# Quadrant products for the block-diagonal state-space matrices of a hybrid decoder layer, with its decode sums, attention split and row moves rearranged

## The reference

```python
x = x + 0.5 * swiglu(rmsnorm(x), w_gate, w_up, w_down)          # D_FF = 5504
z = rmsnorm(x) @ w_in          # q, k, v: 12 heads of 128; u: 1024; gate_a, gate_s: 2048
A = merged dilated attention of three head groups, 4 x 128 wide
# branch B: 64 channel groups of 16 channels, each drives one complex state of 64
bu = einsum('blgc,gpc->lbgp', u, bbar)                           # complex
x_s[l] = a * x_s[l-1] + bu[l]                                    # associative scan
y = Re(einsum('lbgp,gcp->blgc', x_s, c)) + d_skip * u
zs = gelu(y);  s_out = zs * sigmoid(zs @ glu_w + glu_b)
x = x + (sigmoid(gate_a) * (A @ w_attn_branch) + sigmoid(gate_s) * (s_out @ w_ssm_branch)) @ w_out
x = x + 0.5 * swiglu(rmsnorm(x), ...)                            # a second FFN
```

## Time and profile before

| | |
|---|---|
| median of 3 runs | 2301.75 us (2300.42 to 2302.45) |
| the profiled execution, its own time | 2301.55 us |
| its span, first to last instruction | 2299.8 us |
| mean granted TensorE clock | 0.998 |
| PE busy | 2272.1 us, 99% |
| DVE busy | 1404.6 us, 61% |
| ACT busy | 995.0 us, 43% |
| POOL busy | 535.9 us, 23% |

### The profile page before, as it was taken

How to read it: one execution, slowest core, us unless ns; L and a number is a source line. 1 busy time by engine, 2 the same in 40 slices (tenths; PEclk the granted TensorE clock), 3 DMA queues, 4 the chain that set the end, 5 groups by cost and what they waited for, 6 DMA issues and landing times.

```text
span 2299.8 us, 47445 instructions
## 1 busy us (share of the span) xinstructions
PE 2272.1 (99%) x18546; PEld 2255.7 (98%) x18546; DVE 1404.6 (61%) x1414; ACT 995.0 (43%) x1219; POOL 535.9 (23%) x565
## 2 busy tenths in 40 slices
PE   7999999999999999999999999999999999999999
PEld 7999999999999999999999999999999999999998
DVE  6566457775455667886657777655554455544555
ACT  5644333333344543444445555444433344333442
POOL 3795026650000204664405540110000000000000
PEclk9999999999999999999999999999999999999999
DMA  7888777777777688758848865568787777657864
GB/s 209 265 246 284 227 242 248 256 260 246 236 238 224 202 262 260 229 180 284 300 145 307 283 197 186 174 202 270 239 243 224 241 246 250 219 184 222 246 199 139
DMA packets 435222, 535.65 MB, mean 233 GB/s; under 512 B 27744, under 2 KB 415832, under 8 KB 431272
## 3 DMA queue, kind: packets, MB, share of 16 engines
q1 hardware_dynamic: 420224, 511.58, 70.7%
q0 software_dynamic: 3216, 11.75, 1.5%
q10 hardware_dynamic: 11680, 10.91, 1.4%
HBM read 510.95 MB, written 109.10 MB: 270 GB/s over the span
## 4 chain that ended last, share of the span: by engine, by line
PE 87%; DVE 5%; POOL 3%; issue 2%; DMA 1%; ACT 1%; SPq 0%; ACTq 0%; DVEq 0%
PE pa L1313 28%; PE pa L1314 27%; PE pa L1315 27%; DVE w_lo L927 2%; POOL c_exp L1781 1%; DVE head_sd L1088 1%; POOL pre L1777 1%; DMA raw<-in_ffn_w_up 1%; PE pb L1411 1%; PE pb L1586 1%; ACT w_hi L586 1%; PE pb L1571 1%; DVE up_v L1092 0%; DMA raw<-in_ffn_w_gate 0%; DVE xg_lo L934 0%
## 5 line engine op out<-in xcount | busy, mean ns | idle before, releaser
L927 DVE TENSOR_TENSOR w_lo<-raw,w_hi 128x1024 fp32r<-128x1024 f32 x736 | 937.0, 1287 | 643.9 <-ACT w_hi L586 639.3
L1313 PE MATMUL pa<-xg_hi,w_hi 128*128 128x264 f32 x3968 | 1137.5, 287 | 9.1 <-DVE w_lo L927 5.8
L1314 PE MATMUL pa<-xg_lo,w_hi 128*128 128x264 f32 x3968 | 1129.1, 285 | 0.0
L1315 PE MATMUL pa<-xg_hi,w_lo 128*128 128x264 f32 x3968 | 1127.9, 284 | 0.0
L586 ACT ACTIVATE w_hi<-raw 128x1024 fp32r<-128x1024 f32 x736 | 767.3, 1055 | 734.4 <-PE pa L1315 708.4
L1313 PEld LDWEIGHTS pa<-xg_hi,w_hi 128*128 128x128 f32 x3968 | 748.7, 189 | 13.8 <-DVE w_lo L927 6.3
L1314 PEld LDWEIGHTS pa<-xg_lo,w_hi 128*128 128x128 f32 x3968 | 747.3, 188 | 0.6
L1315 PEld LDWEIGHTS pa<-xg_hi,w_lo 128*128 128x128 f32 x3968 | 747.5, 188 | 0.0
L1314 PE MATMUL pa<-act_lo,w_hi 128*128 128x264 f32 x1632 | 463.8, 284 | 0.0
L1313 PE MATMUL pa<-act_hi,w_hi 128*128 128x264 f32 x1632 | 463.5, 284 | 0.0
L1315 PE MATMUL pa<-act_hi,w_lo 128*128 128x264 f32 x1632 | 463.1, 284 | 0.0
(11 more groups left out here) (315 smaller groups left out, 1653.6 us busy)
## 6 DMA issues: line engine op xcount, KB each, us to landing
raw<-in_ffn_w_gate SPq DMA_DIRECT2D x172, 512.0 KB, 4.7
raw<-in_ffn_w_up SPq DMA_DIRECT2D x172, 512.0 KB, 5.5
out_kv_s<-in_cache_kv_w SPq DMA_DIRECT2D x165, 512.0 KB
raw<-in_ffn_w_down SPq DMA_DIRECT2D x160, 512.0 KB, 4.5
raw<-in_w_in SPq DMA_DIRECT2D x152, 512.0 KB, 5.1
raw<-in_w_out SPq DMA_DIRECT2D x32, 512.0 KB, 4.4
tab<-ssm_tab SPq DMA_DIRECT2D x8, 1664.0 KB, 8.9
raw<-in_w_ssm_branch SPq DMA_DIRECT2D x16, 512.0 KB, 3.9
```

Source lines behind the costliest of these rows:

```text
L927: dve.tensor_tensor(w_lo[:, slot], raw[:, slot], w_hi[:, slot].bitcast(f32), ALU.subtract).then_inc(lo_ready, 1)
L1313: pe.matmul(out, wh, hi, start=first, stop=False)
L1314: pe.matmul(out, wh, lo, start=False, stop=False)
L1315: return pe.matmul(out, wl, hi, start=False, stop=last)
```

## The change

- **Tables without zero blocks.** `pre`, `bb_t`, `ca5` and the temporaries have half their columns (POOL: one 128-partition operation where two of 64 stood, one copy `c_cur` for four `c_exp`). PE: 6 transposes per chunk instead of 10; 32 lag calls on 64-row weights of 32 or 16 columns instead of 8 calls. DVE's `kbig` work becomes `lag_table`: two multiply-adds in PSUM and eight small copies, moved behind `act_lo` of the iteration.
- **Products.** B u: 16 calls on 64x64 quadrants for 8 on 128x128. y: 4 full calls for K and 16 quadrant calls for C, for 12 full ones, in banks 2 and 3. The order alternates between the two row halves. PE's `gates_b` is written out instead of looped.
- **`u4` and `yt_v`** have another layout: 48 loads of 16 partitions on SP in `q` and `k` for 24 of 32 partitions; back, 24 moves on SP, 8 on ACT and 8 on POOL, for 14 on SP and 6 on POOL. SP waits for `y_read` before the fifth slab of `attn_branch` and puts 8 moves before each of slabs five, six and seven; ACT puts its 8 between the first two sigmoids.
- **Decode sums** go to bank 0, and wait for `sv_ready` of their chunk; B u waits for `pv_read`.
- **Attention halves.** The 256 prompt columns are split in items 2 and 3 of the last iteration, the 8 sample columns in item 6.
- ACT issues 8 instead of 4 loads of `ssm_d` at the start; ACT's copies out of the B u banks are four instead of two.

```diff
-TB_B, TB_C, TB_K, TB_E, TB_M, TB = 0, 1024, 2048, 2560, 3072, 3328
+TB_B, TB_C, TB_K, TB_E, TB_M, TB = 0, 512, 1024, 1536, 2048, 2304
...
+                            for g in range(2):
+                                row, at = 32 * jj + 16 * g, 64 * (jj % 2) + 16 * s
+                                sync.dma_start(u4[at:at + 16, 2 * (jj // 2) + g::4, col:col + width],
+                                               u_t[row:row + 16, :, part * NB:part * NB + width]).then_inc(u4_loaded, 16)
...
+            moves = [(s, jj, g) for s in range(3) for jj in range(4) for g in range(2)]
+
+            def move(n):
+                for s, jj, g in moves[:n]:
+                    row, at = 32 * jj + 16 * g, 64 * (jj % 2) + 16 * s
+                    sync.dma_start(yt_v[row:row + 16, :, s * NB:(s + 1) * NB],
+                                   u4[at:at + 16, 2 * (jj // 2) + g::4, NS:NS + NB]).then_inc(yt_loaded, 16)
+                del moves[:n]
+
             def attn_branch(i, ph=PH["attn_branch"]):
                 for g in range(4):
+                    if (i, g) == (1, 0):
+                        sync.wait_ge(y_read, SC)
+                    if i == 1:
+                        move(8)
                     put(ph, i, g, cols(A["w_attn_branch"][0], 0, 512, (4 * i + g) * 256))
...
+                            for ri in range(2):
+                                act.activation(sv[:, ri].rearrange("p (a h c) -> p a h c", a=2, h=2), s_ps[:, ri, :, :, 0:NB], ACT.Copy)
+                                act.activation(s_new[:, ri, bass.ds(4 * k, 4), :].rearrange("p (a h) c -> p a h c", h=2),
+                                               s_ps[:, ri, :, :, NB:NB + NS], ACT.Copy)
...
+                    if isinstance(i, int) and i == ph.iters - 1 and j == 2:
+                        act.wait_ge(att_read, NSLOT)
+                        act.activation(att_hi[:, :, 0:NT], att_v[:, :, 0:NT], ACT.Copy).then_inc(att_hi_ready, 1)
                     if isinstance(i, int) and i == ph.iters - 1 and j == 6:
                         act.wait_ge(pv_read, NS)
-                        act.activation(att_hi[:], att_v[:], ACT.Copy).then_inc(att_hi_ready, 1)
+                        act.activation(att_hi[:, :, NT:T], att_v[:, :, NT:T], ACT.Copy).then_inc(att_hi_ready, 1)
...
                     if i == 0:
                         sigmoid(4 * g)
+                        if g == 0:
+                            act.wait_ge(y_read, SC)
+                            for jj in range(4):
+                                for gg in range(2):
+                                    row, at = 32 * jj + 16 * gg, 64 * (jj % 2) + 48
+                                    act.dma_start(yt_v[row:row + 16, :, 3 * NB:4 * NB],
+                                                  u4[at:at + 16, 2 * (jj // 2) + gg::4, NS:NS + NB]).then_inc(yt_loaded, 16)
                         sigmoid(4 * g + 2)
...
+                    if isinstance(i, int) and i == ph.iters - 1 and j in (3, 6):
+                        cols = slice(0, NT) if j == 3 else slice(NT, T)
+                        dve.wait_ge(att_hi_ready, 1 if j == 3 else 2)
+                        dve.tensor_tensor(att_lo[:, :, cols], att_v[:, :, cols], att_hi[:, :, cols].bitcast(f32),
+                                          ALU.subtract).then_inc(att_lo_ready, 1)
...
-                    for t in range(4):
+                    for a in range(2):
                         for ri in range(2):
-                            m = 2 * t + ri
-                            pe.transpose(pb[:, m // 4, (m % 4) * P:(m % 4 + 1) * P], pre[:, ri, t].rearrange("p s g c -> p (s g c)"), ident[:])
+                            m = 2 * a + ri
+                            pe.transpose(pb[:, 0, m * P:(m + 1) * P], pre[:, ri, 2 * a:2 * a + 2].rearrange("p t s c -> p (t s c)"), ident[:])
...
-                            ins = pe.matmul(pb[0:32, 3, t * P:(t + 1) * P], pre[:, ri, t, STEP - 1].rearrange("p g c -> p (g c)"),
-                                            ca5[:, t, ri, 0:P], start=ri == 0, stop=ri == 1)
+                    for wide, ri in ((True, 0), (False, 0), (False, 1), (True, 1)):
+                        for t in range(4):
+                            for g in range(2):
+                                at = slice(64 * g, 64 * g + 64)
+                                if wide:
+                                    ins = pe.matmul(pb[32 * t:32 * t + 32, 2 + g, 0:64], pre[at, ri, t, 2:4].rearrange("p s c -> p (s c)"),
+                                                    ca5[at, t, ri, 0:64], start=ri == 0, stop=ri == 1)
+                                else:
+                                    pe.matmul(pb[32 * t:32 * t + 16, 2 + g, 0:16], pre[at, ri, t, 3], ca5[at, t, ri, 16:32],
+                                              start=False, stop=False)
...
+                        for a in range(2):
+                            def y_out(half, g):
+                                return pb[64 * half:64 * half + 64, 2 + g, P + a * (NS + NB):P + (a + 1) * (NS + NB)]
+                            for g in range(2):
+                                c0 = TB_K + (2 * a + g) * P
+                                pe.matmul(pb[:, 2 + g, P + a * (NS + NB):P + (a + 1) * (NS + NB)], tab[h][:, c0:c0 + P],
+                                          u4[:, 4 * k + 2 * a + g, 0:NS + NB], start=True, stop=False)
                             for ri in range(2):
+                                for g, half in ((0, 0), (1, 1), (0, 1), (1, 0)):
+                                    t = 2 * a + half
+                                    at, c0 = slice(64 * g, 64 * g + 64), TB_C + (2 * t + ri) * 64
+                                    ins = pe.matmul(y_out(half, g), tab[h][at, c0:c0 + 64], xs[at, ri, t, 0:NS + NB],
+                                                    start=False, stop=ri == 1)
...
-                            pe.wait_ge(sv_ready, k)
+                            pe.wait_ge(pv_read, k)
+                        for m in range(4):
+                            for half, g in ((0, 0), (1, 1), (0, 1), (1, 0)):
+                                at, c0 = slice(64 * half, 64 * half + 64), TB_B + m * P + 64 * g
+                                ins = pe.matmul(pb[64 * g:64 * g + 64, half, m * (NS + NB):(m + 1) * (NS + NB)], tab[h][at, c0:c0 + 64],
+                                                u4[at, bass.ds(4 * k + 2 * (m // 2) + g, 1), NS:2 * NS + NB], start=True, stop=True)
...
-                        else:
-                            pe.wait_ge(pv_read, k)
+                        pe.wait_ge(sv_ready, k + 1)
...
-                    for g in range(2):
-                        step(pool.tensor_tensor(pre[64 * g:64 * g + 64, ri, :, :, g, :], b_tmp[64 * g:64 * g + 64, 0],
-                                                b_tmp[64 * g:64 * g + 64, 1], op))
...
-                ins.then_inc(pre_ready, 1)
+                    step(pool.tensor_tensor(pre[:, ri], b_tmp[:, 0], b_tmp[:, 1], op))
+                pool.tensor_copy(c_cur[:], c_in[:, :, i, None, :].to_broadcast([P, 2, 2, 64])).then_inc(pre_ready, 1)
```

More of the change, by code:

```diff
@@ L1624, in _ @@
                             decode(i, j)
-            loop(pe, PH["gates_b"], gates_b, 1, 1)
+            loop(pe, PH["gates_b"], gates_b, 4)
             ph = PH["attn_branch"]
-            pe.wait_ge(att_lo_ready, 1)
+            pe.wait_ge(att_lo_ready, 2)
             for i in range(2):
@@ L1762, in parameters @@
                 pool.wait_ge(e_stored, 16 * SC)
-                step(pool.memset(pre[:], 0.0))
+                step(pool.memset(ca5[:, :, :, 0:16], 0.0))
                 step(pool.memset(kbig[:], 0.0))
+                for t in range(4):
+                    step(pool.tensor_copy(d_mask[32 * t:32 * t + 32, :], ident[32 * t:32 * t + 32, 32 * t:32 * t + 32]))
                 return step
@@ L1911, in _ @@
             for jj in range(4):
[L1912 to L1914 removed]
+                for g in range(2):
+                    row, at = 32 * jj + 16 * g, 64 * (jj % 2)
+                    pool.dma_start(yt_v[row:row + 16, :, NT:T], u4[at:at + 16, 2 * (jj // 2) + g::4, 0:NS]).then_inc(yl_loaded, 16)
             pool.wait_ge(pv_done, NS)
```

152 lines of the change are left out of this document (62 added, 90 removed).

## The result

The changed kernel takes 2286.11 us (median of 4 runs, 2284.30 to 2288.57), the kernel before, run beside it, 2302.10: a ratio of 0.9931, 95% interval 0.9919 to 0.9943, 16 us less. The forecast was 2295.2, in the range 2284 to 2313. The profiled execution took 2285.57 us, its span is 2283.8.

What follows compares the result with a forecast made beforehand. The prediction took PE, busy in 99% of the span, to bound the kernel. Its terms, -3.5 - 8.0 + 1.6 - 4.1 - 3.7 + 10.8 + 0.5 = -6.4, took 2301.55 to 2295.2 us, range 2284 to 2313.

Steps and rivals of the forecast that it cites:

- (a): Table stage: four fewer PE transposes in each of 8 chunks, at 0.109 us each, -3.5 us.
- (b): Table stage: PE's wait for POOL's `c_exp` ahead of the transposes goes, nothing late behind it, -8.0 us.
- (c): Table stage: 64 small lag passes at 0.030 us replace 16 passes, 2.27 us per chunk for 2.07, +1.6 us.
- (d): B u and y in `gates_b`: overlapping quadrant passes at 0.033 us, -4.1 us; break-even at 0.041 us a pass.
- (e): Turn to `attn_branch`: PE's 2.17 us wait for `att_lo` and the clock's fall behind it go, -3.7 us.
- (f): `attn_branch`: SP's blocks of eight moves delay slabs five to seven, and PE waits for emptied groups, +10.8 us.
- (g): Small edits: four more `ssm_d` loads hold ACT's queue at the start, between 0 and 1.8 us, taken as +0.5 us.
- Rival 3: `attn_branch`: the moves don't hurt, as issues are cheap or slabs arrive in time; 2284.4 us, 18%.
- Rivals 1 and 2: Quadrants: 1, loads rule, 0.055 us a pass, 2306.5 us, 18%; 2, no overlap, 0.066 us, lag passes too, 2318.7 us, 15%.
- Rival 4: Table stage: POOL's wait stays in another dress, ACT's copy to `c_t` or `kbig`, +8.0 us, 2303.2 us, 7%.

Runs made afterwards that it cites:

- run 2: The kernel before with POOL's four masked copies that make `c_exp` replaced by one unmasked copy: 2296.40 us.
- run 5: The changed kernel with the 64 lag passes of a chunk ordered tile by tile, each tile's four passes one behind the other: 2292.10 us.
- run 3: The changed kernel with B u's 32 quadrant passes per chunk reordered so that consecutive passes stay on the same quadrant: 2292.22 us.
- run 1: The kernel before with only the attention's halves split early and scratch tile `sv` moved to free memory: 2298.27 us.
- m1: The changed kernel with SP's 24 moves of y placed behind the attention branch's slabs, eight ahead of each of the first three `glu` slabs: 2278.43 us.
- m3: The changed kernel with SP's 24 moves behind the attention branch's slabs and ACT's eight spread two to an item: 2278.12 us.
- b2: b1 with POOL issuing eight of the 32 moves, so that SP has 16 in place of 24: 2270.39 us.
- run 9: The changed kernel with four of the eight `ssm_d` loads on ACT's queue, leaving out D u for half the channels: 2281.92 us.
- b3: b2 with the four `ssm_d` loads issued later, where ACT waits for a slab anyway: 2266.41 us.
- b1: m3 with all of `ssm_d` loaded in four DMAs instead of eight: 2277.87 us.
- run 4: The changed kernel with another quadrant order in B u and y's C products, where neighbours share rows or columns: 2285.97 us.
- m2: The changed kernel with ACT's eight moves spread two to an item behind each item's second sigmoid: 2280.59 us.

## Why the prediction was right, and where it was not

The sign was right and the time lies in the range, near its lower end, 9 us under the forecast. That it lies in the range at all is in part luck: three terms were off by 4 to 10 us each, and their errors partly cancel. By the prediction's own steps:

- **(a) Transposes, -3.5: right.** 0.87 became 0.44.
- **(b) POOL's wait, -8.0: right in mechanism, too large.** Run 2 shows -5.4, and in the changed kernel the stretch is 0.72 shorter per period, not 1.17. What failed is the stretch's floor, 11.65 + 0.19: the return to the weight products costs more (12.09 in run 2's first period, 11.92 in run 5, where PE waits for nothing). And "what is late next is nothing in this stage" was wrong twice: DVE's `kbig` in run 2, `up_v` in the changed kernel, 2.8 us in all.
- **(c) Lag products, +1.6: wrong in sign.** The group fell from 1.88 to 0.79 us, -8.7 in 8 chunks. The step that failed is the price of a pass: 0.030, from six passes whose order I did not ask about. On tiles that alternate, a pass takes 0.012; run 5 makes them share and gets 0.028.
- **(d) Quadrants, -4.1: right in sign and mechanism, too small.** `gates_b` is 14.9 shorter, of which 2.2 are (e): -12.7, in spite of 1.06 us of a new wait for POOL's `xs`. I had p = 0.033 and got 0.021 with the entry in it, 0.016 without. The lone pass was priced rightly, 0.055 to 0.066 for the 0.062 of the traces; the step that failed is the overlap, "if two halves work side by side, p is half": four quadrants do. Run 3 shows that it is overlap: with a quadrant's passes in a row p is 0.044 to 0.049. By my break-even of 0.041 that order would have lost, but B u takes 1.56 and 1.40 us in it and took 1.74 before (y's passes were not run in it). The excursions were priced too high, 0.35 each: B u with an entry takes 0.66 us and without one 0.50.
- **(e) Attention, -3.7: right,** -3.5 in run 1, whose interval is -1.2 to -5.5; in its trace the two stretches are 3.9 us shorter. In the traced run of the changed kernel the clock fell all the same (last section).
- **(f) Moves, +10.8: right in mechanism, too small.** Against run 1's 47.8 us the changed kernel takes 63.0: +15.2. The prediction named the fifth to seventh slabs, the gates and ACT's wait for the DMA, and they are there. Three things it had too small or at nothing. The clock falls three times in the branch, 5.0 us, where one fall of 1.5 was in the sum. The last move releases POOL's reload of x just as SP issues the first `glu` slabs, and PE waits 1.17 and 2.50 us behind them; the prediction has no term for the reload. And ACT's eight moves, which "go through its queue while the engine computes", hold the second sigmoid by 2.47 us; in the changed kernel this is hidden behind slab five, and in m1, where slab five is early, it costs 2.09. With the place of the moves mended 8.0 us are left (m3), with POOL taking eight of them 2.5 (b2).
- **(g) Small edits, +0.5: too small.** The first table comes 2.5 us later, in the mean of the seven kernels with eight loads 1.9 later (324.5) than in the three with four small ones (322.6). The mechanism stands: the queue holds a split back, a slab's buffer comes free late, and its load is late for PE (the wait put down to DVEq, 5.5 us for 3.2). By DVEq's wait, 5.5 us in the changed kernel, 1.6 in run 9 and 0.4 in b3, what the loads hold up depends on how long they take and where they stand; b1 shows that their count alone does not.

With measured sizes: -15.5 in the tables, -12.7, -3.9 (run 1's two stretches), +15.2, +2.5, and -0.9 twice in the stretches between and behind, which no experiment explains, give -16.2, where 16.0 was measured.

**The rivals.** Rival 3, "the moves don't hurt", had 2284.4, the nearest time, for the wrong reason: they hurt more than forecast, and (c) and (d) gain 19 us more. The errors have opposite signs and partly cancel. Rivals 1 and 2 are out for this order of passes; run 3 comes near rival 1's price, p = 0.055, where the passes in a row share a quadrant. Rival 4, POOL's wait in another dress, is seen on DVE's `up_v`, at 2.8 us for the 8.0 it was priced at.

A pass with 64 columns of weights at 0.021 us is less than half of the 53 ns that are the estimate for its load by the rule of the Trainium skill's page "TensorE: Matmul & The Clock Gate", section on LDWEIGHTS. The rows of run 3 (0.049 and 0.044) are near that figure, and so are the 0.062 us of a pass on its own quadrant; those of the changed kernel are not, so as a price of passes on alternating quadrants the rule does not hold here; the measurement decides.

## What to carry to other kernels

Zero blocks of a 128x128 product are worth cutting out as 64x64 quadrants if consecutive passes go to different quadrants. Here B u went from 1.74 us to 0.50 or 0.66 with its loops in one order and to 1.40 or 1.56 in another, and where sums are independent the order is free. A row move between partitions cost its queue 0.5 to 0.8 us here, for 16 partitions as for 32, so halving the rows of a move doubles its cost; count all of them, on the engine that issues them, against what that engine's next instruction is wanted for, and give some to an idle queue. Look also at what the last of them releases: here a transfer of 2112 KB, which goes out beside the slabs or behind them. A wait of PE can cost more than its length, as the clock can fall behind it. A gain on the busiest engine uncovers whatever was just in time behind it.

## What the runs showed of the hardware that I had not expected

- **Passes on different tiles:** 0.021 us for 64x64 weights with 72 columns (0.016 without the entry, 0.062 on one quadrant alone), 0.012 in the mean for 64x32 and 64x16 weights with 64 and 16 columns. Whether neighbours are diagonal or share a row half or a column half made no difference (run 4).
- **The clock behind one and the same wait.** After the 1.04 to 1.09 us for `xs`, the mean granted clock in the first 4 us of `attn_branch` was 0.57 in the changed kernel, m2, run 9 and b1, and 1.00 in runs 4 and 5, m1, m3, b2 and b3, with the same work before it. The windows (us, PE busy, granted clock, DMA share, GB/s) of the changed kernel and of run 4:

```profile
1312.80:1316.80 4.00, 2.94 (x49) 1.00 0.01 4
1316.80:1320.80 4.00, 4.00 (x25) 0.57 0.25 32
```
```profile
1311.50:1315.50 4.00, 2.94 (x49) 1.00 0.00 0
1315.50:1319.50 4.00, 4.00 (x38) 1.00 0.26 35
```

  At 0.57 the 4 us give 1.7 us less work. PE had been equally busy in the 4 us before, in both; what decides isn't shown. It did not decide the time here: in run 4 the first wait for the gates is 4.6 us for 3.4 with a longer fall of the clock behind it, and the stretch to the first `s_hi` product is 63.8 us for 63.0. Behind the 2.17 us wait of the kernel before the clock fell in both traces that have it (0.67 in the first 4 us of the kernel before, 0.62 in run 2).
- **Issue of a move:** 0.60 us on SP and 0.63 on ACT for 16 partitions, as much as for 32 before; 0.53 on POOL. In b2, where POOL issues at the same time, SP's blocks of eight take 6.01 and 6.31 us for 5.1 to 5.3. The bound of 0.35 from ACT's small loads did not apply.
- **Issue of a load** depends on its shape: 0.32 us for 8 rows of two pieces of 64 bytes (eight loads), 0.69 for 8 rows of four such pieces (b1, b2), 0.44 for the 32 rows of 128 bytes of the kernel before. What in the shape decides isn't shown. Eight or four, 2.5 or 2.9 us in all.
